# Head of the expert stage: buffer places, and a gate store cut in two around the first gate load

## What is computed

```python
def peer_ffn(x, w_q, subkeys, u_tab, v_tab):
    q = (xt @ w_q).reshape(n, PEER_HEADS, 2, PEER_QDIM // 2)
    s = jnp.einsum('nhsd,hskd->nhsk', q, subkeys)
    v_top, i_top = lax.top_k(s, PEER_TOPK)
    ...                                   # the best 16 of 16 x 16 pairs per head: eidx, gate
    act = jax.nn.gelu(jnp.einsum('chkd,cd->chk', u_tab[ec], xc))
    return jnp.einsum('chk,chkd->cd', gc * act, v_tab[ec])
```

## Time and profile before

| | us |
|---|---|
| median of 3 runs | 2481.58 |
| lowest, highest | 2476.61, 2482.66 |
| the profiled execution, its own time | 2492.35 |
| its span, first to last instruction | 2490.7 |

### The profile page before, as it was taken

The page is one execution under the profiler, slowest core; times in us unless marked ns, Lnnn a source line. Parts: engine busy times, 40 slices in busy tenths (PEclk is TensorE's granted clock), DMA queues, the critical chain, the costliest instruction groups (busy, mean ns, idle before and its releaser), DMA issues. The chain is left out here.

```text
span 2490.7 us, 36671 instructions
## 1 busy us (share of the span) xinstructions
PE 2196.4 (88%) x11589; PEld 1911.2 (77%) x11589; DVE 1747.6 (70%) x3908; ACT 771.1 (31%) x1376; POOL 721.2 (29%) x653
## 2 busy tenths in 40 slices
PE   7885599777698999985899689999999999999979
PEld 5444389544488989974888678888899999999968
DVE  6845300466322089999999689999889898888852
ACT  2021211354322233331454323333323233232331
POOL 0411311201132344441444222222433333333302
PEclk9987799588898999997999899999999999999999
DMA  5204623412421144440766667778888787878721
GB/s 207 19 24 61 206 81 122 122 56 89 153 77 52 50 172 145 133 146 25 256 186 204 201 246 291 291 291 308 305 286 294 274 309 273 303 274 286 254 89 39
DMA packets 194121, 448.24 MB, mean 180 GB/s; under 512 B 26401, under 2 KB 109602, under 8 KB 184610
## 3 DMA queue, kind: packets, MB, share of 16 engines
q1 hardware_dynamic: 140082, 222.74, 27.3%
q0 software_dynamic: 44288, 156.92, 18.8%
q10 hardware_dynamic: 9648, 67.24, 6.8%
HBM read 394.07 MB, written 54.80 MB: 180 GB/s over the span
## 5 line engine op out<-in xcount | busy, mean ns | idle before, releaser
L2591 PE MATMUL e_ps<-w_hi,v_hi 128*128 128x448 f32 x1024 | 379.8, 371 | 25.2 <-DVE w_lo L2485 15.3
L2591 PE MATMUL e_ps<-w_lo,v_hi 128*128 128x448 f32 x1024 | 378.3, 369 | 0.0
L2591 PE MATMUL e_ps<-w_hi,v_lo 128*128 128x448 f32 x1024 | 378.1, 369 | 0.0
L2591 PEld LDWEIGHTS e_ps<-w_hi,v_hi 128*128 128x128 f32 x1024 | 194.1, 190 | 48.9 <-issue 23.5
L2591 PEld LDWEIGHTS e_ps<-w_hi,v_lo 128*128 128x128 f32 x1024 | 194.1, 190 | 18.0
L2591 PEld LDWEIGHTS e_ps<-w_lo,v_hi 128*128 128x128 f32 x1024 | 194.1, 190 | 17.7
L1571 PE MATMUL e_ps<-x_hi,u_hi 128*128 128x448 f32 x512 | 189.5, 370 | 17.9 <-DVE u_lo L2420 17.9
L1571 PE MATMUL e_ps<-x_lo,u_hi 128*128 128x448 f32 x512 | 189.4, 370 | 0.0
L1571 PE MATMUL e_ps<-x_hi,u_lo 128*128 128x448 f32 x512 | 189.2, 370 | 0.0
L2430 DVE TENSOR_TENSOR hT<-hT,e_ps 128x448 f32<-128x448 f32 x256 | 157.5, 615 | 31.6 <-PE e_ps L2591 31.6
L2324 ACT ACTIVATE v_hi<-v_raw 128x512 fp32r<-128x512 f32 x256 | 157.2, 622 | 68.0 <-PE e_ps L2591 62.3
(11 more groups left out here) (538 smaller groups left out, 5059.5 us busy)
## 6 DMA issues: line engine op xcount, KB each, us to landing
v_raw<-in_v_tab ACTq DMA_DIRECT2D x62, 1024.0 KB, 7.0
u_raw<-in_u_tab SPq DMA_DIRECT2D x64, 512.0 KB, 6.0
gate_scr<-gate_stage SPq DMA_DIRECT2D x14, 2048.0 KB, 9.3
mixT<-gate_scr SPq DMA_DIRECT2D x32, 896.0 KB, 5.9
r_u_raw<-in_u_tab SPq DMA_DIRECT2D x50, 512.0 KB, 3.9
gelu_scr<-mixT SPq DMA_DIRECT2D x32, 448.0 KB, 2.7
acts_and_rows<-gelu_scr SPq DMA_DIRECT2D x16, 896.0 KB, 7.3
m_w_raw<-in_w_mix SPq DMA_DIRECT2D x24, 512.0 KB, 3.5
```

Source lines behind the costliest of these rows:

```text
L2591: mm = nc.tensor.matmul(ps[:, 4 + c % 4, 0:TD], as_r(v[:, c % 4, e]), as_r(w[:, b, e]), start=(e == 0 and n == 0), stop=(e == EG - 1 and n ...
```

## The change

- **Places.** The order of declarations is changed in both stages. `one_hot1`, `one_hot2` and the u buffers of the gate stage now come first (32 KB of each partition), then `gate_stage` (32 KB). In the expert stage `u_hi`, `u_lo`, `v_hi`, `v_lo` take the first 32 KB; `w_raw`, `e_act`, `w_hi0` and, behind them, `w_hi1`, `w_lo1`, `s_sum` fall on `gate_stage`. `w_hi` and `w_lo`, one tensor each before, are two each now.
- **Waits.** ACT and DVE wait for no store at their start.
- **The last store is divided.** The last block stores groups 0 and 1 alone, counted by the new semaphore `gm_first`. SP in the expert stage waits for it and for all earlier stores, loads the gates of group 0, then stores groups 2 to 31, waits for them (and for `spilled_late`), and loads the gates of group 1.
- **The memset** of `s_sum` stands behind the four u gathers on Pool, and waits for the last store.

```diff
@@ gate_matrix_stage
-        iota = sb("iota128", [P, KEYS])
         oh1, oh2 = sb("one_hot1", [P, 8, KEYS]), sb("one_hot2", [P, 8, KEYS])
-        stage, first_picks = sb("gate_stage", [P, 2, NG, TB, EG]), sb("first_picks", [P, 2, TB])
         u_raw, u_hi, u_lo = (sb(f"g_{n}", [P, 2, KD, P]) for n in ("u_raw", "u_hi", "u_lo"))
+
+        k.gate_stage = stage = sb("gate_stage", [P, 2, NG, TB, EG])
+        iota, first_picks = sb("iota128", [P, KEYS]), sb("first_picks", [P, 2, TB])
...
                     sp.wait_ge(copied, 2 * QUADS * i + (QUADS * b + QUADS + 4))
+                    if b == 1 and not ahead:
+                        sp.dma_start(k.d["gate_scr"][0:2, :, NTB - 1, :].rearrange("g p f -> p g f"),
+                                     stage[:, 1, 0:2].rearrange("p g t e -> p g (t e)")).then_inc(k.gm_first, 16)
+                        return
@@ experts_stage
-        w_raw, w_hi, w_lo = sb("w_raw", [P, 2, TD]), sb("w_hi", [P, 2, EG, TD]), sb("w_lo", [P, 2, EG, TD])
-        act_ = sb("e_act", [P, 2, TD])
+        w_raw, act_, w_hi0 = sb("w_raw", [P, 2, TD]), sb("e_act", [P, 2, TD]), sb("w_hi0", [P, EG, TD])
+
+        w_hi1, w_lo1, s_sum = sb("w_hi1", [P, EG, TD]), sb("w_lo1", [P, EG, TD]), sb("s_sum", [P, D])
+        w_lo0 = sb("w_lo0", [P, EG, TD])
+        w_hi, w_lo = (w_hi0, w_hi1), (w_lo0, w_lo1)
...
-            for b in range(2):
-                sp.wait_ge(k.gm_stored[b], 16 + 16 * (NTB // 2))
+            sp.wait_ge(k.gm_first, 16)
+            sp.wait_ge(k.gm_stored[0], 16 + 16 * (NTB // 2))
+            sp.wait_ge(k.gm_stored[1], 16 * (NTB // 2))
             load_gates(0, 0)
 
+            sp.dma_start(k.d["gate_scr"][2:NG, :, NTB - 1, :].rearrange("g p f -> p g f"),
+                         k.gate_stage[:, 1, 2:NG].rearrange("p g t e -> p g (t e)")).then_inc(k.gm_stored[1], 16)
+
             sp.wait_ge(k.spilled_late, 16 + 8 * ONE_HOT_UPS)
+            sp.wait_ge(k.gm_stored[1], 16 + 16 * (NTB // 2))
             load_gates(1, 1)
...
-            pool.memset(s_sum[:], 0.0).then_inc(summed, 1)
             for j in range(EARLY):
                 if j == 0:
 
@@
             for j in range(EARLY):
                 gather("u_rows", EARLY + j, j)
+            pool.wait_ge(k.gm_stored[1], 16 + 16 * (NTB // 2))
+            pool.memset(s_sum[:], 0.0).then_inc(summed, 1)
...
             act.sem_inc(gelu_done, GELU0)
 
-            for b in range(2):
-                act.wait_ge(k.gm_stored[b], 16 + 16 * (NTB // 2))
             for e in range(2):
                 u_high(e, 0)
...
-            for b in range(2):
-                dve.wait_ge(k.gm_stored[b], 16 + 16 * (NTB // 2))
 
             for e in range(2):
                 u_low(e, e)
```

More of the change, by code:

```diff
@@ L2195, in experts_stage @@
         x_rows, s_idx = k.x_rows, k.s_idx
-        s_dots, s_act, s_sum = sb("s_dots", [P, LATE]), sb("s_act", [P, LATE]), sb("s_sum", [P, D])
         row2 = sb("s_rows", [P, 2, D])
+        s_dots, s_act = sb("s_dots", [P, LATE]), sb("s_act", [P, LATE])
         flat_idx = k.idxT[:].rearrange("p n t -> p (n t)")
@@ L2334, in w_high @@
                 act.wait_ge(w_made, EG * s + (e + 1))
-                nc.scalar.activation(as_r(w_hi[:, b, e]), w_raw[:, e % 2], ACT.Copy).then_inc(w_hi_made, 1)
+                nc.scalar.activation(as_r(w_hi[b][:, e]), w_raw[:, e % 2], ACT.Copy).then_inc(w_hi_made, 1)
             def early_step(s, b):
@@ L2484, in w_low @@
                 dve.wait_ge(w_hi_made, EG * s + (e + 1))
-                nc.vector.tensor_tensor(as_r(w_lo[:, b, e]), w_raw[:, e % 2], w_hi[:, b, e], ALU.subtract).then_inc(w_lo_made, 1)
+                nc.vector.tensor_tensor(as_r(w_lo[b][:, e]), w_raw[:, e % 2], w_hi[b][:, e], ALU.subtract).then_inc(w_lo_made, 1)
             def early_step(s, b, turn, first=False):
@@ L2590, in down @@
                         for n, (v, w) in enumerate(((v_hi, w_hi), (v_hi, w_lo), (v_lo, w_hi))):
-                            mm = nc.tensor.matmul(ps[:, 4 + c % 4, 0:TD], as_r(v[:, c % 4, e]), as_r(w[:, b, e]),
+                            mm = nc.tensor.matmul(ps[:, 4 + c % 4, 0:TD], as_r(v[:, c % 4, e]), as_r(w[b][:, e]),
                                                   start=(e == 0 and n == 0), stop=(e == EG - 1 and n == 2))
@@ L2808, in build @@
             "gm_stored", "spilled", "v_loaded", "early_act_loaded"))
+        k.gm_first = k.sem("gm_first")
         k.spilled_late, k.ple_ld = k.sem("spilled_late"), k.sem("ple_loaded")
```

## The result

| kernel | median us | lowest, highest | ratio to before, 95% interval |
|---|---|---|---|
| before, 22 runs | 2483.72 | 2476.61, 2499.68 | |
| after, 22 runs | 2475.48 | 2463.20, 2489.10 | 0.9964 [0.9946, 0.9982] |

The changed kernel is faster by 8.2 us between the medians (0.33%) and by 0.36%, or 8.9 us, by the ratio; the interval of the ratio runs from 4.5 to 13.4 us. I had forecast 2471, 10.9 us less. The profiled execution of after took 2484.53 us, so it lies 9 us above its median, as that of before lay 9 to 11 us above its own.

What follows compares the result with a forecast made beforehand. PE is busiest, but the wait for the 2 MB gate store at the stiff expert stage's head was taken to decide: 13.9 us gained less 3 for the gather's collision, 2481.6 - 10.9 = 2470.7, say 2471 us; range 2463 to 2479.

Steps and rivals of the forecast that it cites:

- The shift of the head: Expert stage's head: ACT starts on u at 1394.3 instead of 1408.20, so the head moves 13.9 us earlier.
- The clock starts cold again: Head's up products: PE restarts at 1.2 GHz after standing 4.0 us, so the 48 products again take 12.34 us.
- Rival 1: Head: PE gets full clock at once, saving 2.5 us, and the gather does not suffer; gain 16.4, 2465 us; chance 0.12.
- The first gate load hidden: Group 0: the load lands at 1401.7, before 1402.9, so w is ready before PE's 1409.1, at no cost.
- The rest of the store lands at 18.8 us: Head: the remaining 30 groups of the gate store land at 1412.3, after 2.2 us of gate load and 2 of pause.
- Rival 2: Head: the rest of the store lands later than 1412.3, delaying v gathers and gate load 1; at 1415, 2474 us; chance 0.18.
- Gate load 1 some 3 us late: Group 1's gates land at 1417.3, 3.0 us late for DVE; 2.95 covered by its existing wait for the v row.
- The memset just fits: Pool: s_sum's memset runs 1412.3 to 1413.3, before the v gather due at 1413.5; no cost, 0.2 us of cover.
- The gather's collision: First v gather meets SP's three 896 KB loads and v_raw; costs 0 to 3.5 us, taken as 3.
- The sum: Whole kernel: 13.9 - 3 = 10.9 us gained, 2481.6 to 2470.7, say 2471 us.
- rival 3: Down matmuls: new buffer places slow each; 4.5 ns eats the whole shift, 8 ns gives 2492 us; chance 0.05.
- rival 4: Expert stage: another condition holds u back, or later parts do not move; gain 0 to 5 us, 2479 us; chance 0.07.

Runs made afterwards that it cites:

- division alone: The changed kernel, but ACT and DVE wait at the head for all of the last store, which stays divided; 2487.44 us, ratio to before 1.0001.
- places alone: The changed kernel, but the last store is whole again and the first gate load waits for it; 2483.25 us, ratio to before 1.0000.
- two loads first: The changed kernel, but gate loads 0 and 1 both precede the rest of the store, and DVE waits for it before group 1; one run 2484.36 us.

## Why the prediction was right, step by step

- **The shift of the head, 13.9 us:** 17.20 - 3.23 = 13.97. Right.
- **The clock starts cold again:** it does, for less time than I took. By stretch in after (engines as in the earlier trace rows; PEclk is the third number from the end):

```profile
1396.00:1398.00 2.00, 2.00 (x7) 1.78 (x6) 2.00 (x5) 0.65 (x2) 1.68 (x2) 0.50 0.97 375
1398.00:1400.00 2.00, 2.00 (x10) 1.82 (x10) 2.00 (x3) 0.58 (x1) 0.67 (x1) 0.94 1.01 364
```

  After 3.4 us at 1.2 GHz the products are at full pace, against 5.4 us in before. The 48 took 11.49 us where I had 12.34, so the down products came at 14.72 and not 15.6. Rival 1, a warm start, fell; a third of its clock gain came true all the same, by an effect that varies from one execution to the next (11.27 in the second profile of before). I had carried one execution's cold stretch over as if it were the kernel's. DVE's dot products, which release the v gather, moved with it.
- **The first gate load hidden:** right. DVE took up w at 1398.38 without a wait, which is 6.7 us behind the store's issue where I had allowed until 9.4.
- **The rest of the store lands at 18.8 us:** 18.75. Rival 2 would have needed it later than 19.0, and fell. That the sum met it so closely is partly luck: the same sum gave 18.7 for the division alone, where the store landed at 17.5; what makes the 1.2 us is open.
- **Gate load 1 some 3 us late, in the shadow of DVE's wait:** DVE waited 3.32 us for it. It was in a shadow on DVE, but not quite on PE, which lost 1.37 us in front of an earlier v_lo. This has no price of its own, since PE meets the next wait sooner by as much.
- **The memset just fits:** it does not quite. The first dot product had ended at 1410.51, and the gather went out at 1411.56, 0.8 us later than it could have. So the 0.85 us of the shorter cold stretch ended here: against before's first profile the gather went out on time (19.86 us against 33.91 - 13.97 = 19.94), against its second profile, whose cold stretch was as short, 1.0 us late (32.83 - 13.97 = 18.86). That much of rival 2 came true, by the memset and not by a late landing.
- **The gather's collision, 0 to 3.5 us, taken as 3:** this is the term that was mis-sized. Issue to use grew from 7.16 to 10.42 us, 3.3, and the second row added its own 1.04, so 4.3. I had weighed two readings of the earlier trace rows as alternatives, a gather that stands behind all that is queued (10.7 us from issue to use, without a term for the second row) or one that takes turns from the start (8.8, with it). Both rows were right, one after the other: it stands behind the first 1 MB, and takes turns from then on, as the 99 packets against 101 did. But the standing phase was already in the 7.2 us of before (4.9 us to the first packet) and did not grow (4.5). What grew is the turns, from 1.4 to 4.9 us, since three loads were still moving. What I should have summed is the old standing phase, the turns behind it, and the second row's wait.
- **The sum,** at PE's mark behind v_lo: 13.97 + 0.1 - 3.3 - 1.0 = 9.8 for the first profiles, where the marks differ by 45.55 - 35.69 = 9.9. For the second profiles it is 13.97 - 0.9 - 3.4 - 1.0 = 8.7, where they differ by 44.36 - 35.67 = 8.7; 0.7 more is gone by the group 1 mark. The measured 8.2 (medians) and 8.9 us (ratio) lie between 9.9 and 8.0. Of the distance to my 10.9 the collision makes 1.3 us, and the long cold stretch of the one profile that I worked from, which made the old head slower than in its second profile, up to 1 more.
- **Placement (rival 3)** fell: the same shapes take the same time, and the places alone have a ratio of 1.0000, with an interval of 5.5 us either way, in which the 13.9 us of this rival have no room. **The change does not do what it says (rival 4)** fell with the first row.

## What to carry to other kernels

A wait that is removed at the head of a long stiff stage is worth what arrives at the first mark behind all of the head's waits: read that mark, in two executions at least, and not the hole. When a store and its loads are put off, list which short gathers of another queue will meet them: here such a gather first stood behind 0.7 to 1.5 MB of other queues, which cost no more than before the change, and then took turns by packet and not by byte, which is where its small packets lost. Two edits that each lift one of two waits in a row may be worth nothing alone, so test them together too.

## What the runs showed that I had not expected

**Two paces of the same matmuls at the same granted clock.** From the first addition of group 16 to that of group 30 the fourteen profiles took either 554.46 us (before, after, division alone, two loads first; all within 0.01) or 543.67 us (the ten others, the second profiles of before and after among them; all within 0.02). That is 10.8 us, more than the whole effect of the change. After and its second profile, one stretch of each (columns as in the earlier trace rows):

```profile
1850.00:1900.00 50.00, 50.00 (x244) 45.41 (x242) 42.18 (x58) 17.61 (x29) 16.42 (x13) 1.00 0.76 261
...
1850.00:1900.00 50.00, 50.00 (x248) 46.34 (x247) 41.08 (x56) 16.48 (x27) 17.40 (x15) 1.00 0.79 278
```

PE is busy throughout and its granted clock is 1.00 in both, but one has 244 matmuls in 50 us and the other 248, a pitch of 0.2067 against 0.2026 us. Both kernels show both paces, so it is no effect of the code.

The choice is not one per execution. Up to about 1760, PE's products come in runs that a stand of PE or a spell at half the clock ends. The fourteen profiles have 209 such runs of 80 or more products that begin before 1760, and each keeps one pace from its first half to its second: 63 the slow one, 146 the fast one. In every profile the last such break of the stage's main part ends between 1749 and 1771, and the 2900 products behind it, some 600 us, keep the pace that they begin with, the slow one in 4 of 14. So the 10.8 us are decided at one restart. What decides it is open.

Besides, the stages ahead of the head ended between 1387.9 and 1397.7 us. Together these two explain why a single run of this kernel says nothing about 10 us, and why the marks, counted from the head, said more than the times.

**A copy beside a memset.** DVE's copy of 128 x 128 took 0.90 us where Pool's memset ran beside it and 0.23 us in after, where it did not. In the kernels that put the memset back it took 0.90 again.
